# A weight block kept on chip, a gather ring of twelve buffers instead of four to six, and an output projection moved behind the first slots

## The chip, the cores and the metric

The kernel runs on one core of one Trainium2 chip. The metric is the device time in microseconds, lower is better. All data is float32.

## What is computed

One decoder layer over 256 tokens of width 1024: a mixer of two attention kinds (MoBA and FoX, 8 heads of 64 each), a cross attention over 256 memory tokens, then a PEER layer. The change touches the seam between the mixer's output projection and the PEER layer, which is this:

```python
def hybrid_mixer(...):
    ...
    o = jnp.concatenate([rmsnorm(o_a...), rmsnorm(o_b...)], axis=-1)
    return o @ w_out                                # 1024 x 1024

def peer_ffn(h, w_query, sub_keys_1, sub_keys_2, expert_down, expert_up):
    # per token: 8 heads, product keys (2 x 128 sub-keys), top 16 experts per head
    qr = (xc @ w_query).reshape(C, 8, 2, 64)
    s1 = einsum('chd,hnd->chn', qr[:, :, 0], sub_keys_1)
    s2 = einsum('chd,hnd->chn', qr[:, :, 1], sub_keys_2)
    v1, i1 = lax.top_k(s1, 16)
    v2, i2 = lax.top_k(s2, 16)
    ...                                             # top 16 of the 256 sums -> eidx, scores
    g = jax.nn.softmax(top_s, axis=-1)
    u = expert_down[eidx]                           # gathered rows of 1024
    a = gelu(einsum('cd,chkd->chk', xc, u))
    vv = expert_up[eidx]                            # gathered rows of 1024
    return einsum('chk,chkd->cd', g * a, vv)
```

Each of the 256 tokens needs 128 experts, each a row of expert_down and one of expert_up. The kernel reads both at once, as one row of 8 KB from `expert_rows`.

## The kernel before

The tokens are two tiles of 128 (T = 2, P = 128). The program has two parts. A list `main` of steps, written out by hand, takes both tiles through the attentions and tile 0 through everything up to its routing; then come 256 slots, 128 for each tile (SPT = 128). Every engine runs the same lists in the same order and does in each step what is its share; they meet only at semaphores.

A slot n handles one expert for each of the 128 tokens of a tile. GpSimd gathers 128 rows of 8 KB into a buffer of the ring (L551; 1.049 MB). VectorE's `dot(n)` multiplies the down half with the normalized token and sums (L1001). ScalarE's `weight(n)` makes gelu (L712), times the gate (L716), and a diagonal matrix `diag` from it (L719). TensorE's `up(n)` multiplies this with the up half and adds to the output in PSUM (L1291: 2 calls that the trace shows as 4 matmuls). That frees the buffer; `up_used` counts it. GpSimd waits for `up_used` of six slots back before it gathers into the same buffer (NS = 6; four of the buffers, NB = 4, lie in QKVB, two in SPARE).

During tile 0's 128 slots, tile 1's remaining stages are run between the slots. `slots` lists them: at which slot a stage stands, or at which four slots its four quarters stand. `after_slot(n, True)` gives TensorE's steps after up(n). `after_slot(n, False)` gives the shares of ScalarE and VectorE: those in OWN at the same slot, all others at the last slot of the stage plus LAG = 4. Names: wout = the mixer's output projection, xT = transposes for the cross attention, xq = its query, xS/xPT/xO = its scores, transposes, values, xo = its output projection, wq = the routing query in two halves of 512 columns, sc = the scores against the sub-keys. A key is (name, tile, half).

TensorE's products of these stages go to two PSUM banks for each of two groups (`v_jobs`, `a_jobs`), used in turn in the order of the steps. `bank_for` makes TensorE wait until the group's job two back has been emptied by ScalarE or VectorE (`freed`). wq, sc, xS, xPT and tile 1's xq are `a_jobs`, emptied by ScalarE; wout, xT, xO, xo are `v_jobs`, emptied by VectorE.

Weights come in blocks of 2 MB (512 columns) into six slots of W; `SLOT` says which, and a block waits until TensorE has done with the block before. The first half of the routing query's weights is loaded twice: early to SPARE (`wq_early`) for tile 0, and again to slot 0 of W for tile 1, after tile 1's wout half 0 (`main` ends with it). SPARE then becomes two buffers of the ring, once tile 0's wq half 0 is done.

The choice of experts for a head (`top_part`, VectorE, 16 parts) is spread over the slots of the head before. ScalarE adds a softmax to it (L704).

Of the kernel before, what the change touches and what calls it, by code (L numbers as in the profile page):

```python
# [18 lines left out]
D = 1024  # L19
# [41 lines left out]
def hybrid_layer(nc, A, out, bias_scratch):  # L61
# [7 lines left out]
    for name, cols in (("w_in", 6), ("w_xk", 2), ("w_xv", 2), ("w_out", 2), ("w_xq", 2), ("w_xo", 2),  # L69
                       ("w_peer_query", 2)):  # L70
        blocks += [(name, b) for b in range(cols)]

    SLOT = dict(zip(blocks, (0, 1, 2, 3, 4, 0, 1, 2, 3, 4, 0, 1, 2, 3, 4, MEM_SLOT, 0, 1)))
# [83 lines left out]
    for part in range(4):  # L157
# [17 lines left out]
    main += rest[1][1:] + [("wq", 0, 0), ("sc", 0, 0), ("sc", 0, 1)] + rest[0]  # L175


    slots = [((0, 1, 3, 4), ("wq", 0, 1)), (8, ("sc", 0, 2)), (9, ("sc", 0, 3)),
             (11, ("xT", 1, 0)), (11, ("xT", 1, 1)), (13, ("root_x", 1, 0)), (16, ("rstd_x", 1, 0)),
# [59 lines left out]
    with ctx:  # L239
# [85 lines left out]
        ROWS = [QKVB[:, 2 * i:2 * i + 2, :].rearrange("p a x -> p (a x)") for i in range(NB)]  # L325
        ROWS += [SPARE[:, 2 * i:2 * i + 2, :].rearrange("p a x -> p (a x)") for i in range(NS - NB)]

# [67 lines left out]
        row_in = [sem(f"row_in{i}") for i in range(NS)]  # L395
# [35 lines left out]
        def col(name, t, i):  # L431
            return {"root_m": i, "root_h": 2 + t, "o_root": 4 + 2 * t + i, "root_x": 8 + 2 * t,
                    "root_p": 9 + 2 * t, "root_y": 12 + t}[name]

# [16 lines left out]
        def _(sp):  # L451
# [63 lines left out]
            for b in (1, 0):  # L515
                load_block("w_peer_query", b)
# [10 lines left out]
        def _(pool):  # L527
# [29 lines left out]
        def _(act):  # L557
# [150 lines left out]
            def weight(n):  # L708

                i, H, k = n % NS, n // PK, n % PK  # L710
                act.wait_ge(dot_done, n + 1)
                nc.scalar.activation(gel[:, i:i + 1], dots[:, i:i + 1], ACT.Gelu, scale=rms("root_p", n // SPT)).then_inc(gelu_done, 1)  # L712
                act.wait_ge(gelu_done, n + 1)
                if k == 0:
                    act.wait_ge(gate_ready, H + 1)
                nc.scalar.activation(wgt[:, i:i + 1], gel[:, i:i + 1], ACT.Copy, scale=GATE[:, H % 3, k:k + 1])\  # L716
                    .then_inc(w_done, 1)
                act.wait_ge(w_done, n + 1)
                nc.scalar.activation(diag[:, i, :], ident[:, :], ACT.Copy, scale=wgt[:, i:i + 1])\  # L719
                    .then_inc(diag_done, 1)  # L720
# [20 lines left out]
        def _(dve):  # L741
# [255 lines left out]
            def dot(n):  # L997

                i = n % NS
                dve.wait_ge(row_in[i], 16 * (n // NS + 1))  # L1000
                nc.vector.tensor_tensor_reduce(out=ROWS[i][:, 0:D], in0=HP[n // SPT][:, :], in1=ROWS[i][:, 0:D],  # L1001
# [36 lines left out]
        def _(pe):  # L1038
# [64 lines left out]
            def step(name, t, i, part=None):  # L1103
# [146 lines left out]
                elif name in ("wq", "wq_first"):  # L1250
                    early = t == 0 and i == 0
                    w, bank = wq_early if early else wblk("w_peer_query", i), ab[AN[key] % 2]
                    if begins:
                        if early:
# [31 lines left out]
            def up(n):  # L1286
# [3 lines left out]
                for b in range(2):  # L1290
                    ins = nc.tensor.matmul(YP[t][:, b * BLK:(b + 1) * BLK], diag[:, i, :],  # L1291
                                           ROWS[i][:, D + b * BLK:D + (b + 1) * BLK], start=False,
# [39 lines left out]
```

## Time and profile before

| | |
|---|---|
| three runs | 932.72, 936.67, 942.36 us (median 936.67) |
| the profiled execution | 935.35 us, of which the span is 933.5 us |
| TensorE (PE) busy | 812.0 us, 87% of the span |
| VectorE (DVE) busy | 556.3 us, 60% |
| ScalarE (ACT) busy | 443.2 us, 47% |
| GpSimd (POOL) busy | 242.9 us, 26% |
| mean DMA rate | 339 GB/s over the span |

Slots run from about 276 us to 928 us. Engines: PE = TensorE matmul, PEld = its weight load, DVE = VectorE, ACT = ScalarE, POOL = GpSimd, SPq = SyncE's queue of transfers. A busy engine is not by itself the bound; what counts is which wait ends last in a stretch. In a row of the timeline "[0.77 <-ACT weights L699]" says that the engine was idle for 0.77 us before this, and that ScalarE's instruction of line 699 ended it.

### The profile page before, as it was taken

The numbers are of one execution on the slowest core, as the hardware profiler recorded it, in microseconds if no ns is written. First come the engines' busy times: TensorE is split into PE (matmuls) and PEld (weight loads), VectorE is DVE, ScalarE is ACT, GpSimd is POOL, SyncE is SP. The second block draws the span as 40 slices with busy tenths as digits, with TensorE's granted clock in tenths as the row PEclk, the third lists the DMA queues.
The fourth block names the chain that finished last, engine by engine and source line by source line (L and its number), as shares of the span: only waits on it lengthen the run. The fifth ranks groups of instructions, "written<-read, shape, count | busy, mean of one in ns | idle before, by whom it ended". The sixth has DMA issues, their size and how long they took to land.

```text
span 933.5 us, 9388 instructions
## 1 busy us (share of the span) xinstructions
PE 812.0 (87%) x3163; PEld 453.6 (49%) x3163; DVE 556.3 (60%) x1342; ACT 443.2 (47%) x1085; POOL 242.9 (26%) x267
## 2 busy tenths in 40 slices
PE   5999999999989899888899899977778787777885
PEld 3999897587555455344343456332223222222222
DVE  4464343212356766777768657776666666676543
ACT  4445555333324555565536644564553535445343
POOL 0000000000023333434333333433334343333430
PEclk9999999998999999999999999999999999999999
DMA  9749642052079999999999999999999999999994
GB/s 345 230 82 384 225 159 90 1 186 86 1 304 412 414 403 419 413 398 422 421 421 421 422 416 411 414 420 422 421 421 421 410 410 421 421 422 421 418 421 204
DMA packets 63299, 316.33 MB, mean 339 GB/s; under 512 B 7891, under 2 KB 10004, under 8 KB 30484
## 3 DMA queue, kind: packets, MB, share of 16 engines
q0 software_dynamic: 36864, 268.45, 69.6%
q1 hardware_dynamic: 26340, 47.28, 15.1%
q8 instruction: 25, 0.41, 0.2%
q14 instruction: 22, 0.18, 0.0%
q10 hardware_dynamic: 48, 0.01, 0.0%
HBM read 313.10 MB, written 2.62 MB: 338 GB/s over the span
## 4 chain that ended last, share of the span: by engine, by line
PE 49%; DMA 32%; ACT 10%; DVE 6%; issue 2%; SPq 0%; POOL 0%; POOLq 0%
DMA qkvb<-in_expert_rows,expert_idx 18%; DMA spare<-in_expert_rows,expert_idx 13%; PE y L1291 12%; PE v_bank L1291 6%; PE h_psum L1068 5%; PE v_bank L1061 4%; PE a_bank L1061 4%; PE a_bank L1068 4%; PE v_bank L1068 4%; PE h_psum L1061 3%; DVE qkvb L1001 3%; ACT diag L719 2%; ACT L712 2%; PE v_bank L1156 2%; DVE spare L1001 2%
## 5 line engine op out<-in xcount | busy, mean ns | idle before, releaser
L551 POOL DMA_INDIRECT qkvb<-in_expert_rows,expert_idx x172 | 161.7, 940 | 537.9 <-DVE expert_idx L984 262.6
L712 ACT ACTIVATE gelu<-dots,stat 128x1 f32<-128x1 f32 x256 | 75.2, 294 | 310.6 <-DVE dots L1001 310.1
L1291 PE MATMUL v_bank<-qkvb,diag 128*128 128x512 f32 x344 | 171.0, 625 | 47.8 <-ACT diag L719 47.8
L1291 PE MATMUL y<-qkvb,diag 128*128 128x512 f32 x344 | 162.7, 611 | 21.0 <-ACT diag L719 21.0
L1001 DVE CUSTOM_DVE_ANT_0 qkvb<-a_bank,qkvb 128x1024 f32<-128x1024 f32 x86 | 105.2, 1223 | 72.4 <-DMA qkvb<-in_expert_rows,expert_idx 72.3
L1001 DVE CUSTOM_DVE_ANT_0 qkvb<-h_psum,qkvb 128x1024 f32<-128x1024 f32 x86 | 105.0, 1223 | 62.4 <-DMA qkvb<-in_expert_rows,expert_idx 62.3
L1291 PEld LDWEIGHTS v_bank<-qkvb,diag 128*128 128x128 f32 x344 | 60.4, 192 | 157.9 <-ACT diag L719 110.1
L551 POOL DMA_INDIRECT spare<-in_expert_rows,expert_idx x84 | 79.7, 949 | 132.1 <-PE y L1291 67.9
L1291 PEld LDWEIGHTS y<-qkvb,diag 128*128 128x128 f32 x344 | 62.5, 192 | 101.4 <-issue 57.5
L719 ACT ACTIVATE diag<-ident,wgt 128x128 f32<-128x128 f32 x256 | 102.7, 401 | 8.3
L1291 PE MATMUL v_bank<-spare,diag 128*128 128x512 f32 x168 | 81.7, 613 | 21.6 <-ACT diag L719 21.6
L1291 PE MATMUL y<-spare,diag 128*128 128x512 f32 x168 | 79.7, 611 | 7.0 <-ACT diag L719 7.0
L716 ACT ACTIVATE wgt<-gelu,gates 128x1 f32<-128x1 f32 x256 | 75.4, 295 | 8.4
L1001 DVE CUSTOM_DVE_ANT_0 spare<-a_bank,spare 128x1024 f32<-128x1024 f32 x42 | 51.4, 1224 | 35.7 <-DMA spare<-in_expert_rows,expert_idx 35.7
L1001 DVE CUSTOM_DVE_ANT_0 spare<-h_psum,spare 128x1024 f32<-128x1024 f32 x42 | 51.3, 1221 | 25.4 <-DMA spare<-in_expert_rows,expert_idx 25.3
L1291 PEld LDWEIGHTS v_bank<-spare,diag 128*128 128x128 f32 x168 | 29.2, 189 | 73.3 <-ACT diag L719 50.1
L808 DVE TENSOR_TENSOR weights_r<-weights,spare_r 128x2048 fp32r<-128x2048 f32 x20 | 45.8, 2289 | 29.8 <-ACT spare_r L620 29.8
L1291 PEld LDWEIGHTS y<-spare,diag 128*128 128x128 f32 x168 | 30.6, 193 | 46.1 <-issue 27.2
L620 ACT CAST spare_r<-weights 128x2048 fp32r<-128x2048 f32 x20 | 38.0, 1898 | 22.2 <-PE v_bank L1068 21.3
L1061 PEld LDWEIGHTS a_bank<-x_and_h,weights 128*128 128x128 f32 x320 | 39.2, 193 | 11.2 <-issue 11.2
L1061 PE MATMUL a_bank<-x_and_h,weights 128*128 128x128 f32 x320 | 39.3, 276 | 0.8 <-ACT weights L699 0.8
L1068 PE MATMUL h_psum<-weights_r 128*128 128x256 f32 x128 | 36.1, 282 | 0.0
(200 smaller groups left out, 1135.4 us busy)
## 6 DMA issues: line engine op xcount, KB each, us to landing
weights<-in_w_in SPq DMA_DIRECT2D x6, 2048.0 KB, 13.5
weights<-in_w_xk SPq DMA_DIRECT2D x2, 2048.0 KB, 16.8
weights<-in_w_xv SPq DMA_DIRECT2D x2, 2048.0 KB, 17.8
weights<-in_w_out SPq DMA_DIRECT2D x2, 2048.0 KB, 8.8
weights<-in_w_xq SPq DMA_DIRECT2D x2, 2048.0 KB, 7.8
weights<-in_w_xo SPq DMA_DIRECT2D x2, 2048.0 KB, 11.0
weights<-in_w_peer_query SPq DMA_DIRECT2D x2, 2048.0 KB, 15.3
qkvb<-in_expert_rows,expert_idx POOLq DMA_INDIRECT x172, 10.0
```

The source lines that it names most:

```text
L551: pool.indirect_dma_start(ROWS[n % NS], None, expert_rows, bass.IndirectOffsetOnAxis(ap=IDX[:, H % 3, k:k + 1], axis=0))\
L620: act.copy(WH_r[t % 2], half_block(t, W)).then_inc(high_ready, 1)
L712: nc.scalar.activation(gel[:, i:i + 1], dots[:, i:i + 1], ACT.Gelu, scale=rms("root_p", n // SPT)).then_inc(gelu_done, 1)
L716: nc.scalar.activation(wgt[:, i:i + 1], gel[:, i:i + 1], ACT.Copy, scale=GATE[:, H % 3, k:k + 1])\
L719: nc.scalar.activation(diag[:, i, :], ident[:, :], ACT.Copy, scale=wgt[:, i:i + 1])\
L808: nc.vector.tensor_tensor(half_block(t, W_r), half_block(t, W), WH_r[t % 2].bitcast(f32), ALU.subtract).then_inc(low_ready, 1)
L1001: nc.vector.tensor_tensor_reduce(out=ROWS[i][:, 0:D], in0=HP[n // SPT][:, :], in1=ROWS[i][:, 0:D], scale=1.0, scalar=0.0, op0=ALU.mult, op ...
L1061: ins = nc.tensor.matmul(bank[:, lo:lo + n], lhs(k), rhs(k), start=(k == 0), stop=(k == chunks - 1))
L1068: ins = nc.tensor.matmul(bank[:, lo:lo + n], a(k), b(k), start=(k == 0 and p == 0), stop=(k == KC - 1 and p == 2))
L1156: ins = nc.tensor.matmul(bank[:, 0:nk], Q[lo:lo + HD, t, c, :], K[lo:lo + HD, 0:t + 1, c, :], start=True, stop=i < NH)
L1291: ins = nc.tensor.matmul(YP[t][:, b * BLK:(b + 1) * BLK], diag[:, i, :], ROWS[i][:, D + b * BLK:D + (b + 1) * BLK], start=False, stop=n % ...
```

## The change

Three edits. (1) The first half of the routing query's weights stays in SPARE for both tiles, and its second load goes. (2) The ring has twelve buffers: four in QKVB, and eight that become free in the course of tile 0's slots, two each after tile 1's wout half 0 (slot 0 of W), xq half 1 (second halves of slots 2 and 3 of W), the last xO (the memory keys and values), and wq half 0 (SPARE). Which buffer a gather takes is worked out in advance: the one that is free first. (3) Tile 1's wout half 0 moves from the end of `main` to slots 3 to 6. Tile 0's wq half 1 moves from slots 0 to 4 to slots 7 to 13, its scores from 8 and 9 to 18 and 19, xT from 11 to 12. Since dots, diag and the like still have six places, VectorE and ScalarE get a wait each for the place.

By these rules gathers 4 to 10 take the buffer of four slots back, 11 and 12 the two behind wout, 13 to 39 that of six slots back, 42 to 72 eight, 75 to 113 ten, 116 and on twelve.

```diff
@@ -68,9 +68,9 @@
-        blocks += [(name, b) for b in range(cols)]
-
-    SLOT = dict(zip(blocks, (0, 1, 2, 3, 4, 0, 1, 2, 3, 4, 0, 1, 2, 3, 4, MEM_SLOT, 0, 1)))
+        blocks += [(name, b) for b in range(cols) if (name, b) != ("w_peer_query", 0)]
+
+    SLOT = dict(zip(blocks, (0, 1, 2, 3, 4, 0, 1, 2, 3, 4, 0, 1, 2, 3, 4, MEM_SLOT, 1)))
@@ -172,11 +172,11 @@
-    main += rest[1][1:] + [("wq", 0, 0), ("sc", 0, 0), ("sc", 0, 1)] + rest[0]
-
-
-    slots = [((0, 1, 3, 4), ("wq", 0, 1)), (8, ("sc", 0, 2)), (9, ("sc", 0, 3)),
-             (11, ("xT", 1, 0)), (11, ("xT", 1, 1)), (13, ("root_x", 1, 0)), (16, ("rstd_x", 1, 0)),
+    main += rest[1][1:] + [("wq", 0, 0), ("sc", 0, 0), ("sc", 0, 1)]
+
+
+    slots = [((3, 4, 5, 6), ("wout", 1, 0)), ((7, 9, 11, 13), ("wq", 0, 1)), (18, ("sc", 0, 2)), (19, ("sc", 0, 3)),
+             (12, ("xT", 1, 0)), (12, ("xT", 1, 1)), (13, ("root_x", 1, 0)), (16, ("rstd_x", 1, 0)),
              ((19, 21, 23, 25), ("xq", 1, 0)), ((27, 29, 31, 33), ("xq", 1, 1))]
@@ -431,6 +428,26 @@
+        ROWS = [QKVB[:, 2 * i:2 * i + 2, :].rearrange("p a x -> p (a x)") for i in range(NB)]
+        ROWS += [W[:, wslot("w_out", 0), 2 * D * i:2 * D * (i + 1)] for i in range(2)]
+        ROWS += [W[:, wslot("w_xq", b), 2 * D:4 * D] for b in range(2)]
+        ROWS += [KM[:, :, :].rearrange("p c x -> p (c x)"), VM[:, :, :].rearrange("p a x -> p (a x)")]
+        ROWS += [SPARE[:, 2 * i:2 * i + 2, :].rearrange("p a x -> p (a x)") for i in range(2)]
+
+
+        last_of = dict(zip(range(NB, len(ROWS)), [st for st in (("wout", 1, 0), ("xq", 1, 1), ("xO", 1, XH_N - 1),
+                                                                ("wq", 1, 0)) for _ in range(2)]))
+        leaves = {st: at[-1] if isinstance(at, tuple) else at for at, st in slots}
+        free_from = {i: leaves[st] for i, st in last_of.items()}
+        BUF, USE, TAKES_FROM = [], [], []
+        for n in range(T * SPT):
+            before = {i: max([m for m in range(n) if BUF[m] == i], default=None) for i in range(len(ROWS))}
+            at = {i: before[i] if before[i] is not None else free_from.get(i, i - NB) for i in range(len(ROWS))}
+            i = min(at, key=lambda i: (at[i], i))
+            BUF.append(i)
+            USE.append(BUF.count(i))
+            TAKES_FROM.append(before[i])
@@ -512,8 +529,7 @@
-            for b in (1, 0):
-                load_block("w_peer_query", b)
+            load_block("w_peer_query", 1)
@@ -544,13 +560,13 @@
-                if n == NB:
-                    pool.wait_ge(a_full, AN[("wq", 0, 0)] + 1)
-                if n >= NS:
-                    pool.wait_ge(up_used, n - NS + 1)
-                pool.indirect_dma_start(ROWS[n % NS], None, expert_rows,
+                if TAKES_FROM[n] is not None:
+                    pool.wait_ge(up_used, TAKES_FROM[n] + 1)
+                elif BUF[n] in last_of:
+                    pool.wait_ge(*full(last_of[BUF[n]]))
+                pool.indirect_dma_start(ROWS[BUF[n]], None, expert_rows,
                                         bass.IndirectOffsetOnAxis(ap=IDX[:, H % 3, k:k + 1], axis=0))\
-                    .then_inc(row_in[n % NS], 16)
+                    .then_inc(row_in[BUF[n]], 16)
@@ -716,6 +732,8 @@
+                if n >= NS:
+                    act.wait_ge(up_used, n - NS + 1)
                 nc.scalar.activation(diag[:, i, :], ident[:, :], ACT.Copy, scale=wgt[:, i:i + 1])\
                     .then_inc(diag_done, 1)
@@ -997,8 +1015,11 @@
                 i = n % NS
-                dve.wait_ge(row_in[i], 16 * (n // NS + 1))
-                nc.vector.tensor_tensor_reduce(out=ROWS[i][:, 0:D], in0=HP[n // SPT][:, :], in1=ROWS[i][:, 0:D],
+                rows = ROWS[BUF[n]][:, 0:D]
+                dve.wait_ge(row_in[BUF[n]], 16 * USE[n])
+                if n >= NS:
+                    dve.wait_ge(gelu_done, n - NS + 1)
+                nc.vector.tensor_tensor_reduce(out=rows, in0=HP[n // SPT][:, :], in1=rows,
                                                scale=1.0, scalar=0.0, op0=ALU.mult, op1=ALU.add,
                                                accum_out=dots[:, i:i + 1]).then_inc(dot_done, 1)
@@ -1248,10 +1269,9 @@
-                    early = t == 0 and i == 0
-                    w, bank = wq_early if early else wblk("w_peer_query", i), ab[AN[key] % 2]
+                    w, bank = wq_early if i == 0 else wblk("w_peer_query", i), ab[AN[key] % 2]
...
```

## Rows read from the trace of the kernel before

**Rows 1.** The page: engines' busy time, and the gathers' DMA queue.
```profile
PE 812.0 (87%) x3163; PEld 453.6 (49%) x3163; DVE 556.3 (60%) x1342; ACT 443.2 (47%) x1085; POOL 242.9 (26%) x267
...
q0 software_dynamic: 36864, 268.45, 69.6%
```

**Rows 2.** Stretches: PE, PEld, DVE, ACT, POOL busy, PE clock, DMA share, GB/s.
```profile
320.00:330.00 10.00, 10.00 (x21) 4.38 (x20) 6.63 (x18) 5.63 (x15) 4.37 (x5) 0.83 0.99 379
...
600.00:740.00 140.00, 108.28 (x223) 39.36 (x223) 96.80 (x245) 71.37 (x189) 51.70 (x55) 0.99 1.01 421
```

**Rows 3.** Timeline, VectorE: dots of gathers 5, 8, 19, 20, 21, 39, 255.
```profile
285.53 1.23 DVE L1001 CUSTOM_DVE_ANT_0 spare<-h_psum,spare 128x1024 f32<-128x1024 f32 x1 [0.22 <-DMA spare<-in_expert_rows,expert_idx]
...
298.42 1.22 DVE L1001 CUSTOM_DVE_ANT_0 qkvb<-h_psum,qkvb 128x1024 f32<-128x1024 f32 x1 [1.19 <-DMA qkvb<-in_expert_rows,expert_idx]
...
325.51 1.22 DVE L1001 CUSTOM_DVE_ANT_0 qkvb<-h_psum,qkvb 128x1024 f32<-128x1024 f32 x1 [0.89 <-DMA qkvb<-in_expert_rows,expert_idx]
...
328.00 1.22 DVE L1001 CUSTOM_DVE_ANT_0 qkvb<-h_psum,qkvb 128x1024 f32<-128x1024 f32 x1 [0.73 <-DMA qkvb<-in_expert_rows,expert_idx]
...
332.50 1.23 DVE L1001 CUSTOM_DVE_ANT_0 qkvb<-h_psum,qkvb 128x1024 f32<-128x1024 f32 x1 [2.90 <-DMA qkvb<-in_expert_rows,expert_idx]
...
377.31 1.22 DVE L1001 CUSTOM_DVE_ANT_0 qkvb<-h_psum,qkvb 128x1024 f32<-128x1024 f32 x1 [0.57 <-DMA qkvb<-in_expert_rows,expert_idx]
...
923.11 1.22 DVE L1001 CUSTOM_DVE_ANT_0 qkvb<-a_bank,qkvb 128x1024 f32<-128x1024 f32 x1 [1.21 <-DMA qkvb<-in_expert_rows,expert_idx]
```

**Rows 4.** Timeline, SyncE's queue: the two loads of routing weights.
```profile
261.28 14.62 SPq L463 DMA_DIRECT2D weights<-in_w_peer_query  x2
```

**Rows 5.** Timeline: one round of a buffer in the second tile.
```profile
905.78 1.22 DVE L1001 CUSTOM_DVE_ANT_0 qkvb<-a_bank,qkvb 128x1024 f32<-128x1024 f32 x1 [1.26 <-DMA qkvb<-in_expert_rows,expert_idx]
...
908.16 1.98 PE L1291 MATMUL v_bank<-qkvb,diag 128*128 128x512 f32 x4 [0.51 <-ACT diag L719]
...
910.41 0.94 POOL L551 DMA_INDIRECT qkvb<-in_expert_rows,expert_idx  x1 [1.55 <-PE v_bank L1291]
```

**Rows 6.** Issues of gathers 0, 20, 21; landing times of the 0.5 MB loads.
```profile
265.07 1.09 POOL L551 DMA_INDIRECT qkvb<-in_expert_rows,expert_idx  x1 [262.63 <-DVE expert_idx L984]
...
321.32 0.94 POOL L551 DMA_INDIRECT qkvb<-in_expert_rows,expert_idx  x1 [4.47 <-PE y L1291]
...
324.23 0.94 POOL L551 DMA_INDIRECT qkvb<-in_expert_rows,expert_idx  x1 [1.97 <-PE y L1291]
...
DMA to landing us min/median/max: 3.3/3.8/4.2
```

**Rows 7.** Timeline, TensorE: end of main, the first slots, and after a wait.
```profile
267.18 1.26 PE L1277 MATMUL a_bank<-subkeys_t,scaled_gffn 64*128 64x128 f32 x12 [0.57 <-ACT scaled_gffn L689]
...
278.52 3.40 PE L1291 MATMUL y<-qkvb,diag 128*128 128x512 f32 x4 [3.01 <-ACT diag L719]
...
318.56 5.40 PE L1291 MATMUL y<-qkvb,diag 128*128 128x512 f32 x8 [2.91 <-ACT diag L719]
```

**Rows 8.** Chain that ended last: start, us; a v_bank quarter, an a_bank quarter, two up-projections.
```profile
458.66 1.72 PE v_bank L1061 x4
...
540.10 1.78 PE a_bank L1061 x16
541.89 3.44 PE y L1291 x8
```

**Rows 9.** Timeline around slot 112: dot, copy of scores, the quarter that waits.
```profile
562.42 1.23 DVE L1001 CUSTOM_DVE_ANT_0 spare<-h_psum,spare 128x1024 f32<-128x1024 f32 x1 [1.23 <-DMA spare<-in_expert_rows,expert_idx]
...
564.65 0.57 ACT L699 COPY weights<-a_bank 128x512 f32<-128x512 f32 x1
...
565.36 2.02 PE L1061 MATMUL a_bank<-x_and_h,weights 128*128 128x128 f32 x16 [0.77 <-ACT weights L699]
```

**Rows 10.** Timeline, VectorE: two dots that waited longer, gathers 124 and 227.
```profile
593.12 1.22 DVE L1001 CUSTOM_DVE_ANT_0 spare<-h_psum,spare 128x1024 f32<-128x1024 f32 x1 [1.62 <-DMA spare<-in_expert_rows,expert_idx]
...
853.61 1.22 DVE L1001 CUSTOM_DVE_ANT_0 spare<-a_bank,spare 128x1024 f32<-128x1024 f32 x1 [1.88 <-DMA spare<-in_expert_rows,expert_idx]
```

More of the change, by code:

```diff
@@ L323, in hybrid_layer @@
         sc = Ssb[:, 1, :].rearrange("p (a x) -> p a x", a=2)
-        ROWS = [QKVB[:, 2 * i:2 * i + 2, :].rearrange("p a x -> p (a x)") for i in range(NB)]
-        ROWS += [SPARE[:, 2 * i:2 * i + 2, :].rearrange("p a x -> p (a x)") for i in range(NS - NB)]
         wq_early = SPARE[:, :, :].rearrange("p a x -> p (a x)").rearrange("p (k c) -> p k c", k=KC)
@@ L394, in hybrid_layer @@
         top_in, top_exp, idx_ready, gate_ready = sem("top_in"), sem("top_e"), sem("idx_ready"), sem("gate_ready")
-        row_in = [sem(f"row_in{i}") for i in range(NS)]
+        row_in = [sem(f"row_in{i}") for i in range(NB + 8)]
         dot_done, gelu_done, diag_done, up_used = (sem("dot_done"), sem("gelu_done"), sem("diag_done"),
@@ L1250, in step @@
                 elif name in ("wq", "wq_first"):
-                    early = t == 0 and i == 0
-                    w, bank = wq_early if early else wblk("w_peer_query", i), ab[AN[key] % 2]
+                    w, bank = wq_early if i == 0 else wblk("w_peer_query", i), ab[AN[key] % 2]
                     if begins:
-                        if early:
+                        if i == 0:
                             pe.wait_ge(ld_early, 16)
@@ L1291, in up @@
                     ins = nc.tensor.matmul(YP[t][:, b * BLK:(b + 1) * BLK], diag[:, i, :],
-                                           ROWS[i][:, D + b * BLK:D + (b + 1) * BLK], start=False,
+                                           ROWS[BUF[n]][:, D + b * BLK:D + (b + 1) * BLK], start=False,
                                            stop=n % SPT == SPT - 1)
```

## The prediction

> **What bounds the kernel now.** The page comes first. TensorE is busy for 87% of the span and looks like the bound, but queue 0, which carries the expert rows, has moved 268.45 MB of the 316 MB [rows 1]. The table of stretches says more. From 600 to 740 us the share of the 16 DMA engines is 1.01 at 421 GB/s while TensorE is busy for 108 of 140 us [rows 2]: there the transfers bound the kernel. So I follow the landings, not an engine. A slot's dot product on VectorE starts where its gather lands, whenever the idle time before it ends with the DMA. A gather is 128 rows of 8 KB, 1.049 MB; at 421 GB/s that is 2.49 us, and gathers 19 and 20 land 2.49 us apart [rows 3]. I call 2.486 us the pitch and measure each landing by its offset, the time less 2.486 n:
>
> - gather 5: 285.53 - 12.4 = 273.1
> - gather 8: 298.42 - 19.9 = 278.5
> - gather 19: 325.51 - 47.2 = 278.3
> - gather 21: 332.50 - 52.2 = 280.3
> - gather 39: 377.31 - 97.0 = 280.4
> - gather 255: 923.11 - 634.0 = 289.1 [rows 3]
>
> A loop at its limit would keep the offset. All that any edit to the loop can win is in those 16.0 us: 5.4 from gather 5 to 8, 2.0 at gather 21, 8.7 after gather 39. From the last dot to the end of the span are 10.4 us, which the change leaves alone. The profiled execution took 935.35 us (1.3 below the median 936.67, 1.85 above its span 933.5).
>
> **The change, part by part.**
>
> The second load of the first half of the routing weights goes. SyncE issues both halves' loads in one group, 14.62 us from the first issue [rows 4]; the second runs beside gathers 5 to 8. Its 2.097 MB at 421.8 GB/s are 4.97 us, nearly all of the 5.4. Term: -5.4, if nothing else leaves the DMA engines idle there.
>
> Four buffers instead of six until slot 6. The two SPARE buffers now hold weights up to slot 103. By the diff's list gathers 4 to 10 each wait for the up-projection four slots back, 11 and 12 for the last quarter of the output projection in slot 6, 13 and on for that six slots back (eight from gather 42, ten from 75, twelve from 116). One round of a buffer: from the dot to the next issue 910.41 - 905.78 = 4.63 us [rows 5], then issue to landing. For the latter in an empty queue the trace has no clean row. Gather 20, issued 4.2 us before gather 19 landed, landed on pitch, 6.7 us after issue; gather 21, issued 3.8 us before gather 20, took 8.27 us and came 2.0 late [rows 3, 6]. A plain 0.5 MB load took 3.3 us at least [rows 6], so with another half megabyte (1.24 us) 4.5 is the lower end. I take 6.5, close to the row that kept its pitch, with 4.5 and 8.3 as ends. A round is then 4.63 + 6.5 = 11.1 us against 4 x 2.486 = 9.9.
>
> In times: gather 0 is issued at 265.07 [rows 6] and lands at 271.6, the next three follow on pitch. TensorE goes idle at 267.18 + 1.26 = 268.4, so its first up-projection runs slowly: 3.40 us, as now after a similar idle time, for 1.98 [rows 5, 7], 1.4 us more. Gather 4 is issued at 271.6 + 4.63 + 1.4 = 277.6 and lands at 284.1, 2.6 late. From slot 3 TensorE has an up-projection (3.44 / 2 = 1.72) and a quarter of the moved output projection (1.72, the row of a like one) in each slot [rows 8], 3.44 us for a pitch of 2.49: slot 4's up-projection ends at 288.4, slot 6's at 295.3, slot 6's quarter at 297.0. Gather 10 is issued at 295.5, lands at 302.0, 5.5 late, and gather 11 at 304.5. Offset 271.6 + 5.6 = 277.2, against 278.3 now. So the opening gives 1.1 us, not 5.4. Starting slot 0 without the 7.1 us of this projection ahead of it is in these times already. The matmuls move and none goes; VectorE's one add moves with them, to slot 10, where VectorE waits for landings anyway.
>
> A wait that the diff does not name. ScalarE's and VectorE's share of a stage follows LAG = 4 slots after TensorE's. The second routing half moves to slots 7 to 13, its two score products to slots 18 and 19. ScalarE thus empties the first one's bank after slot 22. But TensorE's step ("xq", 1, 0) in slot 19 writes that same bank (two jobs later, and there are two banks), and waits for it. Now the scores lie in slots 8 and 9, and the copy is done by slot 13. The trace has one wait of the kind: scores in slot 108, copied in slot 112, bank wanted in slot 111; TensorE resumes 565.36 - 562.42 = 2.94 us after the dot of slot 112 starts, 0.77 us idle [rows 9]. One slot ahead costs little; three slots ahead is two pitches more. Queued behind it are up-projections 20 to 22, and gathers 26 and on wait for those. Gather 22 lands at 277.2 + 54.7 = 331.9, TensorE resumes at 334.8 after some 6 us idle. It then has the quarter of xq (1.78) and up-projection 20 (1.72) before gather 26 goes out. After 2.9 us idle at 316 eight matmuls took 5.40 us where others take 3.44, and the granted clock of the stretch is 0.83 [rows 2, 7, 8], between full 2.4 GHz and a share at 1.2: I take 1.8 us more. So 340.1, issue at 340.3, landing at 346.8; on pitch it would be 341.8. Lost: 5.0 us. After that two slots cost TensorE 3.44 + 1.78 = 5.22 us [rows 8] against 4.97, so the backlog holds to slot 33, some five pairs, 1.2 us. Offset at gather 39: 277.2 + 5.0 + 1.2 = 283.4, against 280.4 now: **+3.0 us**.
>
> The Trainium skill, "DMA: Bandwidth & Descriptors", section "Anatomy of one DMA", fits a DMA issued from GpSimd as about 2.0 us + bytes / 436 GB/s, 4.4 us for this gather. No row here shows one so short. By it the gather round would be 9.0 us, under four pitches, and the bank wait would leave about 3 us; the sum would come out at 930. This is the second rival below, priced there from rows.
>
> The wider ring. Of the 8.7 us after gather 39, two transfers of 0.5 MB (the final gain, the first tile's output) are 2 x 1.24 = 2.5 by the pitch, and stay. The other 6.2 are small steps of at most 1.1 us. About half, 3.5, lie in the first tile, beside its stages, where TensorE or ScalarE gives a buffer back late; the one at gather 124 (593.12, idle 1.62 us) stands in [rows 10]. The rest lie in the second tile, which has no stages; gather 227's (853.61) stands there, 1.0 late, and a longer queue can't mend what no late buffer caused. Bounds: 0 to 3.5, and with no such distinction 6.2. I take two thirds of the first tile's: **-2.3 us**.
>
> At nothing: the new waits of ScalarE for up_used before writing diag and of VectorE for gelu_done, since six places of diag and dots were covered by the six buffers before, and ScalarE is half idle; GpSimd's waits, since each is for something older than the gather before; the first tile's experts for a head are ready nine slots ahead, which only caps the twelve at nine across a head's end.
>
> Sum: 935.35 + 3.0 - 2.3 = **936 us**.
>
> **Rivals.**
>
> 1. The bank wait is not there or is covered (ScalarE reaches slot 22 while TensorE is still behind). For it: TensorE's backlog from slots 3 to 13. Against: by my times TensorE has caught up by slot 19. Price: -6.2, so 930.
> 2. A gather into an empty queue lands after 4.5 us, not 6.5. It enters three times, in two rounds of four buffers and once after the bank wait: 936 - 6 = 930. Against it stand gathers 20 and 21.
> 3. Slower. It takes 8.3 us, as gather 21: 936 + 3 x 1.8 = 941; with the ring giving nothing back, 944. The one mechanism is DMA engines idle between slots 4 and 33. It is slower by over 1% (9.4 us) only from about 9.4 us per landing, which no row shows.
> 4. The wide ring holds the pitch throughout, every step outside the two transfers was a late issue: 16.0 - 2.5 = 13.5 us off, 922. Against: the steps of the second tile [rows 10].
>
> **How the numbers follow.** Chances: forecast 0.40, rival 1 0.16, rival 2 0.14, rival 3 0.22, rival 4 0.08. The predicted time is the forecast's. Range 928 to 943: below are rival 4 and little else, above the worst part of rival 3; it takes in 930 and 941 with two or three us for the median of a few runs, since the runs of before lie between 932.72 and 942.36. About 1% is what a measurement can tell from no change. Under 927.3: rival 4 and the edge of rivals 1 and 2, 0.13. Over 946: 0.09. Between: 0.78.
>
> **What would show it.** Gather 8's offset near 275 to 276 and the next ones rising to 277 by gather 11 (opening). In slot 19, near 328, TensorE idle about 6 us until ScalarE's copy of scores of shape 128x512; then DMA share below 1 in 335 to 345 and a landing about 5 us late at gather 26. Offsets level across slots 37 to 64 and at gather 124. The last dot 10.4 us before the end. Wrong if slot 19 shows no wait, if gathers 4 and 8 land on pitch, or if offsets after gather 39 rise by over 9 us or under 5.

## The result: slower by 0.7%

| | median | lowest to highest | runs |
|---|---|---|---|
| before | 935.84 us | 931.33 to 943.62 | 20 |
| after | 943.15 us | 938.44 to 948.40 | 20 |

The ratio is 1.0074, 95% interval 1.0056 to 1.0092, so about 7 us more. The profiled execution took 940.76 us with a span of 939.0. The median lies 7 us above the forecast of 936 and 0.15 us past the upper end of its range (943). One execution each of e2, e4 and e10 below, and one of before beside e1 to e4, was over 10% slower than the rest; the ratios leave these out.

The slots' landings show where. These are dots of the kernel after, on VectorE's timeline (start in us, duration, what ended the idle time before it): gathers 0, 4, 11, 25, 26, 27, 30, 32, 39 and 255.

```profile
268.97 1.23 DVE L1022 CUSTOM_DVE_ANT_0 qkvb<-h_psum,qkvb 128x1024 f32<-128x1024 f32 x1 [5.94 <-DMA qkvb<-in_expert_rows,expert_idx]
...
280.90 1.22 DVE L1022 CUSTOM_DVE_ANT_0 qkvb<-h_psum,qkvb 128x1024 f32<-128x1024 f32 x1 [2.33 <-DMA qkvb<-in_expert_rows,expert_idx]
...
302.71 1.22 DVE L1022 CUSTOM_DVE_ANT_0 weights<-h_psum,weights 128x1024 f32<-128x1024 f32 x1
...
337.46 1.23 DVE L1022 CUSTOM_DVE_ANT_0 qkvb<-h_psum,qkvb 128x1024 f32<-128x1024 f32 x1 [0.87 <-DMA qkvb<-in_expert_rows,expert_idx]
...
344.94 1.23 DVE L1022 CUSTOM_DVE_ANT_0 qkvb<-h_psum,qkvb 128x1024 f32<-128x1024 f32 x1 [5.52 <-DMA qkvb<-in_expert_rows,expert_idx]
...
349.14 1.23 DVE L1022 CUSTOM_DVE_ANT_0 qkvb<-h_psum,qkvb 128x1024 f32<-128x1024 f32 x1 [2.42 <-DMA qkvb<-in_expert_rows,expert_idx]
...
358.30 1.23 DVE L1022 CUSTOM_DVE_ANT_0 weights<-h_psum,weights 128x1024 f32<-128x1024 f32 x1 [1.83 <-DMA weights<-in_expert_rows,expert_idx]
...
365.16 1.22 DVE L1022 CUSTOM_DVE_ANT_0 qkvb<-h_psum,qkvb 128x1024 f32<-128x1024 f32 x1 [2.84 <-DMA qkvb<-in_expert_rows,expert_idx]
...
382.53 1.22 DVE L1022 CUSTOM_DVE_ANT_0 qkvb<-h_psum,qkvb 128x1024 f32<-128x1024 f32 x1 [0.58 <-DMA qkvb<-in_expert_rows,expert_idx]
...
928.55 1.22 DVE L1022 CUSTOM_DVE_ANT_0 qkvb<-a_bank,qkvb 128x1024 f32<-128x1024 f32 x1 [1.23 <-DMA qkvb<-in_expert_rows,expert_idx]
```

The offset (time less 2.486 n) is 275.4 at gather 11 and still 275.3 at gather 25, as in [rows 3] a landing every 2.486 us. It is 280.3 at gather 26, 282.0 at 27, 283.7 at 30 and 285.6 at 32. Then it is level to gather 39 and reaches 294.6 at the last.

The instructions before the slots are nearly the same in all kernels, yet the first gather goes out at a different time in each execution: at 265.07 us in the profile of before [rows 6], at 262.38 here, between 260.8 and 268.1 in the others. I therefore compare the offset less the time of the first issue, which I call the lag:

| lag, us | gather 19 | 25 | 32 | 39 | 255 | rise from 39 to 255 |
|---|---|---|---|---|---|---|
| before | 13.2 | 15.3 | 15.3 | 15.3 | 24.1 | 8.8 |
| after | 13.0 | 12.9 | 23.2 | 23.2 | 32.2 | 9.0 |

So 10.3 us go between gathers 25 and 32. At gather 25 the kernel after was still 2.4 us ahead of before, so 7.9 remain at gather 39, beside the 7 us of the medians. Each lag is from one profiled execution, and it varies: e3 and e6 below have this kernel's instructions up to slot 18 and show 15.3 and 13.4 at gather 19 for the 13.0 here. A difference of 2 us between two profiles is therefore no more than a hint; the 10.3 us are a rise within one.

Around slot 19 the timeline of TensorE and its neighbours reads as follows: the second score product, the dot of slot 22, ScalarE's copy of the first score product, the quarter of the cross-attention query that waits for it, the next up-projections, and GpSimd's issue of gather 26.

```profile
327.39 1.16 PE L1297 MATMUL a_bank<-subkeys_t,scaled_gffn 64*128 64x128 f32 x8
...
330.05 1.23 DVE L1022 CUSTOM_DVE_ANT_0 qkvb<-h_psum,qkvb 128x1024 f32<-128x1024 f32 x1 [0.59 <-DMA qkvb<-in_expert_rows,expert_idx]
...
332.28 0.57 ACT L715 COPY x_and_h<-a_bank 128x512 f32<-128x512 f32 x1
...
332.99 3.76 PE L1082 MATMUL a_bank<-x_and_h,weights 128*128 128x128 f32 x16 [4.45 <-ACT x_and_h L715]
...
336.54 4.24 PE L1311 MATMUL y<-qkvb,diag 128*128 128x512 f32 x8
...
339.33 0.94 POOL L567 DMA_INDIRECT qkvb<-in_expert_rows,expert_idx  x1 [10.66 <-PE y L1311]
```

TensorE stood idle for 4.45 us, until ScalarE had made the copy that comes after the dot of slot 22. It resumed 2.94 us after that dot started, as in [rows 9]; there it had to wait for the next slot only, here for the one three slots on. Then the quarter took 3.76 us for the usual 1.95. GpSimd had nothing free to gather into for 10.66 us, and the last of its gathers had landed 1.9 us before it issued the next. The stretches (PE, PEld, DVE, ACT, POOL busy, PE clock, DMA share, GB/s) show the DMA engines idle for a third of the time, a granted clock of 0.77 on average, and, less expected, that they move only 384 GB/s in the 30 us behind it, at a share of 1.00:

```profile
330.00:345.00 15.00, 12.01 (x47) 8.35 (x48) 7.44 (x18) 4.93 (x15) 2.33 (x3) 0.77 0.64 244
345.00:375.00 30.00, 30.00 (x142) 19.24 (x141) 16.70 (x45) 10.44 (x32) 11.66 (x13) 1.00 1.00 384
```

### The profile page after: what moved, and what is told of

Same layout as the page of the kernel before. It is cut to its first block, busy times and chain, and to the rows that moved or that the text cites. A ratio compares the mean times of both kernels' runs of the same rounds, so it can differ in the third digit from the quotient of the medians.

```text
span 939.0 us, 9886 instructions
## 1 busy us (share of the span) xinstructions
PE 813.3 (87%) x3163; PEld 453.9 (48%) x3163; DVE 556.5 (59%) x1342; ACT 443.0 (47%) x1085; POOL 242.8 (26%) x267
## 4 chain that ended last, share of the span: by engine, by line
DMA 44%; PE 42%; ACT 6%; DVE 4%; issue 3%; POOL 1%; SPq 0%; DVEq 0%; POOLq 0%
DMA weights<-in_expert_rows,expert_idx 29%; DMA spare<-in_expert_rows,expert_idx 11%; PE y L1311 10%; PE h_psum L1089 5%; PE a_bank L1089 4%; PE v_bank L1082 4%; PE v_bank L1089 4%; DMA qkvb<-in_expert_rows,expert_idx 3%; PE a_bank L1082 3%; PE v_bank L1311 3%; PE h_psum L1082 3%; PE v_bank L1177 2%; PE y L1198 1%; ACT diag L737 1%; DMA weights<-in_w_in 1%
## 5 line engine op out<-in xcount | busy, mean ns | idle before, releaser
L567 POOL DMA_INDIRECT qkvb<-in_expert_rows,expert_idx x110 | 103.7, 942 | 422.1 <-DVE expert_idx L1002 261.3
L1311 PE MATMUL y<-qkvb,diag 128*128 128x512 f32 x264 | 126.7, 613 | 15.0 <-ACT diag L737 14.9
L567 POOL DMA_INDIRECT weights<-in_expert_rows,expert_idx x90 | 84.9, 943 | 149.1 <-PE y L1311 69.5
L1311 PE MATMUL v_bank<-weights,diag 128*128 128x512 f32 x172 | 89.0, 641 | 27.4 <-ACT diag L737 27.4
L1311 PE MATMUL v_bank<-qkvb,diag 128*128 128x512 f32 x176 | 86.0, 616 | 20.0 <-ACT diag L737 20.0
L1311 PE MATMUL y<-weights,diag 128*128 128x512 f32 x188 | 91.3, 612 | 12.6 <-ACT diag L737 12.6
L1022 DVE CUSTOM_DVE_ANT_0 weights<-h_psum,weights 128x1024 f32<-128x1024 f32 x47 | 57.5, 1223 | 31.2 <-DMA weights<-in_expert_rows,expert_idx 31.1
L1022 DVE CUSTOM_DVE_ANT_0 qkvb<-a_bank,qkvb 128x1024 f32<-128x1024 f32 x44 | 53.9, 1224 | 37.2 <-DMA qkvb<-in_expert_rows,expert_idx 37.2
L1022 DVE CUSTOM_DVE_ANT_0 weights<-a_bank,weights 128x1024 f32<-128x1024 f32 x43 | 52.6, 1224 | 37.6 <-DMA weights<-in_expert_rows,expert_idx 37.6
L1311 PE MATMUL v_bank<-spare,diag 128*128 128x512 f32 x80 | 39.2, 614 | 8.4 <-ACT diag L737 8.4
L1082 PEld LDWEIGHTS a_bank<-x_and_h,weights 128*128 128x128 f32 x256 | 32.6, 200 | 12.9 <-issue 12.9
## 6 DMA issues: line engine op xcount, KB each, us to landing
weights<-in_w_in SPq DMA_DIRECT2D x6, 2048.0 KB, 13.4
weights<-in_w_xk SPq DMA_DIRECT2D x2, 2048.0 KB, 17.3
```

The source lines that it names most:

```text
L567: pool.indirect_dma_start(ROWS[BUF[n]], None, expert_rows, bass.IndirectOffsetOnAxis(ap=IDX[:, H % 3, k:k + 1], axis=0))\
L1022: nc.vector.tensor_tensor_reduce(out=rows, in0=HP[n // SPT][:, :], in1=rows, scale=1.0, scalar=0.0, op0=ALU.mult, op1=ALU.add, accum_out=d ...
L1082: ins = nc.tensor.matmul(bank[:, lo:lo + n], lhs(k), rhs(k), start=(k == 0), stop=(k == chunks - 1))
```

## The experiments

All are float32 kernels of the same work. Each was timed in five rounds beside the kernel before; a ratio is to that, with its 95% interval. The lags are read from each one's profile as above, one profile for each.

| run | ratio | lag at 19 | 25 | 32 | 39 | rise 39 to 255 |
|---|---|---|---|---|---|---|
| e1, scores early | 1.0050 (1.0027 to 1.0073) | 18.6 | 20.8 | 20.8 | 20.8 | 10.3 |
| e2, before, scores late | 1.0059 (1.0033 to 1.0085) | 13.0 | 13.0 | 21.4 | 22.0 | 8.2 |
| e3, xq four later | 0.9981 (0.9953 to 1.0009) | 15.3 | 15.9 | 16.3 | 16.2 | 10.7 |
| e4, wout in main | 1.0006 (0.9978 to 1.0034) | 13.1 | 13.6 | 13.6 | 13.6 | 10.9 |
| e5, e4 with six buffers | 0.9998 (0.9979 to 1.0018) | 14.1 | 15.7 | 17.3 | 17.3 | 14.0 |
| e6, after with six buffers | 1.0078 (1.0051 to 1.0105) | 13.4 | 13.3 | 22.2 | 22.1 | 11.6 |
| e7, e4, add after the dots | 0.9954 (0.9925 to 0.9983) | 9.4 | 11.2 | 12.3 | 12.3 | 9.2 |
| e8, e7 with six buffers | 0.9964 (0.9939 to 0.9990) | 8.4 | 9.9 | 9.9 | 9.8 | 11.0 |
| e9, e8 less the added waits | 0.9957 (0.9932 to 0.9981) | 8.6 | 9.5 | 9.5 | 9.4 | 10.7 |
| e10, before with the added waits | 0.9999 (0.9976 to 1.0022) | 13.4 | 15.6 | 15.6 | 15.5 | 13.1 |

### The bank wait, taken away and put in

Run e3_xq_four_later moves the step that waits:

```diff
-             ((19, 21, 23, 25), ("xq", 1, 0)), ((27, 29, 31, 33), ("xq", 1, 1))]
+             ((23, 25, 27, 29), ("xq", 1, 0)), ((31, 33, 35, 36), ("xq", 1, 1))]
```

> The changed kernel with the other end of the wait moved: tile 1's cross-attention query from slots 19 to 33 to slots 23 to 36, four buffers at the start and the late scores kept. Theory 1: no wait (the bank is copied after slot 22), offset at gather 39 about 276 to 278, time 934 to 936. Rivals A and B: 943.

Measured: 934.59 us, ratio 0.9981; against the changed kernel's 1.0074 that is 0.9%, 8 to 9 us. After the second score product TensorE goes on at once (its timeline; then the stretch as above):

```profile
333.11 1.16 PE L1297 MATMUL a_bank<-subkeys_t,scaled_gffn 64*128 64x128 f32 x8
...
343.02 1.95 PE L1082 MATMUL a_bank<-x_and_h,weights 128*128 128x128 f32 x16
```
```profile
330.00:345.00 15.00, 13.75 (x54) 7.56 (x54) 10.19 (x25) 9.43 (x23) 5.62 (x6) 1.00 1.01 421
```

The DMA engines are full in those 15 us, and the lag rises by 0.3 us from gather 25 to 32 instead of 10.3. The offset at gather 39 was 281.9, not 276 to 278: the first gather went out 3.3 us later than in the profile of after, and the same opening lost 2.4 us more. The opening with four buffers, the late scores and the ring of twelve are all still there.

Run e2_before_scores_late does the same part alone in the kernel before:

```diff
-    slots = [((0, 1, 3, 4), ("wq", 0, 1)), (8, ("sc", 0, 2)), (9, ("sc", 0, 3)),
+    slots = [((0, 1, 3, 4), ("wq", 0, 1)), (18, ("sc", 0, 2)), (19, ("sc", 0, 3)),
```

> The kernel before with one thing of the change alone: the scores moved from slots 8 and 9 to 18 and 19; reload, six buffers and everything else stay. Theory 1: TensorE waits 4 to 6 us in slot 19, gathers 26 to 32 come late, plus 8 to 10 us, ratio 1.009 to 1.011. Rivals A and B: no more than 1 us, ratio within 1.001.

In this kernel root_x writes its unused squares over the query (both use XS) before the late scores read it, so heads 4 to 7 of tile 0 choose other experts; the amount of work is the same. Measured: 942.25 us, ratio 1.0059. TensorE waits for the bank in the same place and as long:

```profile
336.50 3.75 PE L1061 MATMUL a_bank<-x_and_h,weights 128*128 128x128 f32 x16 [4.42 <-ACT x_and_h L699]
```

The lag rises by 8.4 us from gather 25 to 32. The time rose by 5.5 us (3.1 to 8.0 by the interval), less than the 8 to 10 expected. The profile of before has a step of 2.0 us at gather 21 [rows 3] that this one lacks (lag 13.0 at gather 25, for 15.3), so that 6.7 us remain at gather 39. Taking the wait out of the changed kernel gives back 8 to 9 us, and putting it into the one before costs 5.5: the wait, with what follows it, is the cause of the slowdown.

### Why the scores had been moved

Run e1_scores_early puts them and the routing half back into the changed kernel:

```diff
-    slots = [((3, 4, 5, 6), ("wout", 1, 0)), ((7, 9, 11, 13), ("wq", 0, 1)), (18, ("sc", 0, 2)), (19, ("sc", 0, 3)),
+    slots = [((3, 4, 5, 6), ("wout", 1, 0)), ((0, 1, 3, 4), ("wq", 0, 1)), (8, ("sc", 0, 2)), (9, ("sc", 0, 3)),
```

> The changed kernel with one thing put back: the second routing half in slots 0, 1, 3, 4 and its scores in slots 8 and 9, as before the change. Theory 1 (the bank wait of slot 19 and the backlog behind it cost the loop about 10 us: the offset rose from 275.35 at gather 25 to 285.6 at gather 32): no wait in slot 19, offset at gather 39 near 276 to 278 (slots 3 and 4 now carry two quarters each), time about 934 to 936, ratio to before 0.998 to 1.001. Rival A (the opening with four buffers is the loss, the wait is covered): within 1 us of the changed kernel's 943. Rival B (twelve buffers, or rows in other places of the memory, make the landings slower): also 943.

Measured: 942.59 us. The wait is gone, but the 934 to 936 did not come, and by time alone this run would have spoken for the four buffers. The lag says what happened: it is 18.6 already at gather 19 and 20.8 at gather 25, and flat after that. Slots 3 and 4 now hold two quarters each, and with four buffers GpSimd waits for each up-projection behind them (timeline; the issues of gathers 8 and 9 with the quarters ahead):

```profile
290.10 1.88 PE L1311 MATMUL y<-qkvb,diag 128*128 128x512 f32 x4
291.82 1.88 PE L1082 MATMUL v_bank<-weights,x_and_h 128*128 128x512 f32 x4
292.26 0.94 POOL L567 DMA_INDIRECT qkvb<-in_expert_rows,expert_idx  x1 [4.28 <-PE y L1311]
293.54 1.95 PE L1082 MATMUL a_bank<-x_and_h,weights 128*128 128x128 f32 x16
295.32 1.88 PE L1311 MATMUL y<-qkvb,diag 128*128 128x512 f32 x4
297.04 1.88 PE L1082 MATMUL v_bank<-weights,x_and_h 128*128 128x512 f32 x4
297.48 0.94 POOL L567 DMA_INDIRECT qkvb<-in_expert_rows,expert_idx  x1 [4.28 <-PE y L1311]
```

Two issues 5.2 us apart where a landing takes 2.49: two quarters and an up-projection occupy TensorE for that long. In e3, with the quarters spread as in the changed kernel, the lag at gather 11 is 15.4, here 18.6. So in this opening the quarters have to be spread, and the spreading is what put the scores late. One loss was exchanged for another that is nearly as large. Whether six buffers would ride over the double quarters was not run.

### Where the reload's 5 us are

Run e4_wout_in_main undoes the third edit: the projection back ahead of slot 0, wq, scores and xT at their old slots; no reload, six buffers from the start and twelve later.

```diff
-    main += rest[1][1:] + [("wq", 0, 0), ("sc", 0, 0), ("sc", 0, 1)]
+    main += rest[1][1:] + [("wq", 0, 0), ("sc", 0, 0), ("sc", 0, 1)] + rest[0]
...
+        leaves["wout", 1, 0] = -1
```

> The changed kernel with its third edit undone: the output projection stays ahead of slot 0, the second routing half in slots 0 to 4, scores in 8 and 9, xT in 11. The reload stays away, the ring has six buffers from the start and twelve later. Theory 1 together with the 5.0 us of the reload: no wait, offset at gather 8 about 3 to 4 below that of the kernel before, time 931 to 933, ratio 0.995 to 0.997. If the reload only filled DMA time that the opening leaves idle anyway: 935 to 936, ratio 1.0. Rival B: above 936.

Measured: 936.82 us, ratio 1.0006, by the ratio the second of the three cases. Its lag at gather 19 is 13.1, that of before 13.2: the reload was a transfer in time that the opening leaves idle otherwise. The stretch behind the first slots shows it, e4 first and then before:

```profile
280.00:300.00 20.00, 20.00 (x91) 12.79 (x90) 15.12 (x50) 9.28 (x24) 5.62 (x6) 0.92 0.93 338
280.00:300.00 20.00, 20.00 (x93) 12.98 (x92) 13.05 (x44) 8.19 (x21) 5.69 (x7) 0.94 1.02 412
```

VectorE's add of the projection stands ahead of dot 0, so the first up-projection starts at 279.13 after 3.01 us of idle time and takes 3.29 us, as in [rows 7], and gather 6 waits for it. Run e7_add_after_dots moves that one add:

```diff
             for st in whole(main, 3):
-                step(*st)
+                if st != ("wout", 1, 0):
+                    step(*st)
...
                 dot(n)
+                if n == 3:
+                    step("wout", 1, 0)
```

> Run e4_wout_in_main with one more edit: VectorE's add of the output projection comes after the dot of slot 3 and not ahead of slot 0, so that the first dots start as their gathers land (near 272) and TensorE goes from the projection (ends near 275.5) straight into slot 0, without idle time or low clock. In e4 the freed time of the reload was lost in the opening: offset less the first issue 13.1 at gather 19, as before the change. If the late start of the first round does this: gather 6 is issued near 277.5 and not 282.7, offset less first issue 9 to 11 at gather 19, time 2 to 4 us below e4. If six buffers beside the quarters of slots 0 to 4 do it: same as e4 within 1 us.

Measured: 932.51 us, ratio 0.9954, the fastest with e8 and e9. The projection (7.13 us) goes into slot 0's up-projection without a gap and without the low clock, the first dots run as their gathers land, and gather 6 is issued at 273.98, 13.2 us after gather 0; in before it was 17.1 after. The lag at gather 19 is 9.4.

```profile
264.09 7.13 PE L1086 MATMUL v_bank<-weights,x_and_h 128*128 128x512 f32 x16
...
267.58 1.23 DVE L1023 CUSTOM_DVE_ANT_0 qkvb<-h_psum,qkvb 128x1024 f32<-128x1024 f32 x1 [6.15 <-DMA qkvb<-in_expert_rows,expert_idx]
...
271.06 1.88 PE L1315 MATMUL y<-qkvb,diag 128*128 128x512 f32 x4
...
273.98 0.93 POOL L568 DMA_INDIRECT qkvb<-in_expert_rows,expert_idx  x1 [0.31 <-issue]
```

So the two edits together, no reload and the later add, are worth some 4 us, and the first alone nothing that the time shows. What the later add would give with the reload kept was not run. An estimate from these profiles: in e7 the lag is 6.7 us at gather 3 and 9.4 from gather 4 on, since gather 4 waits for the projection's buffer; with the reload's 4.97 us on top of the 6.7 instead it would be 11.7, against 13.2 in before. By that the later add would win 1.5 us of the 3.8 and the reload's absence 2.3.

### The ring

Three pairs differ only in the ring: e5, e6 and e8 have six buffers throughout where e4, the changed kernel and e7 have twelve.

```diff
-            i = min(at, key=lambda i: (at[i], i))
+            i = min([i for i in at if i < 6], key=lambda i: (at[i], i))
```

> Run e4_wout_in_main with the ring held at six buffers throughout (four in QKVB, two in slot 0 of W); all else equal. Theory 2 (a ring beyond six buffers saves nothing, and lets the offset rise faster: 10.9 us from gather 39 to 255 in e4 against 8.7 and 8.2 in the two kernels with six buffers): the rise is 7 to 9 us, time 1 to 3 us below e4, ratio to before 0.996 to 0.999. Theory 3 (the ring of twelve keeps the transfers fed across the stages): the rise is 12 us or more, time above e4's.

> The changed kernel with the ring held at six buffers; the opening with four, the late scores and the bank wait kept. Both theories expect the wait of slot 19 and some 10 us of offset from gather 25 to 32. Theory 2: rise after gather 39 of 7 to 9 us, time the same as the changed kernel or up to 2 us below, 941 to 943. Theory 3: 945 or more.

> Both edits of e5 and e7: wout in main, its add after the dot of slot 3, six buffers throughout. If both act: 3 to 6 us below e4, ratio to before 0.993 to 0.996, the fastest of all. If neither: as e4, ratio 1.000.

Measured, six buffers against twelve: 935.67 against 936.82 us (ratios 0.9998 and 1.0006), 944.07 against 943.15 (1.0078 and 1.0074), 932.51 against 932.51 (0.9964 and 0.9954). In the times the ring makes no difference that can be told, but with intervals of about 0.2 to 0.3% on each ratio, 2 to 3 us, a gain of the size forecast isn't excluded either. In the profiles the rise from gather 39 to 255 is 14.0 against 10.9, 11.6 against 9.0, 11.0 against 9.2, so it is 1.8 to 3.2 us smaller with twelve buffers, all three times against theory 2, which is out. That the ring saves these 1.8 to 3.2 us is not shown. One profile of each stands behind it; kernels with the same ring of twelve and the same slots after 39 lie between 9.0 and 10.9 (after, e1, e4, e7); and of the profiled executions those of e5 and e6 took 3.1 and 3.8 us more than their medians, those of e4 and after 0.6 and 2.4 us less.

### What the rise after gather 39 is

In the five kernels with twelve buffers it comes, in the second tile, in steps of about 1 us at the same gathers each time (142, 167, 189, 213, 238), with 22 us of issued gathers queued; a late issue can't be the cause there. Here are gathers 167, 189 and 213 of the kernel after:

```profile
707.03 1.22 DVE L1022 CUSTOM_DVE_ANT_0 weights<-a_bank,weights 128x1024 f32<-128x1024 f32 x1 [1.52 <-DMA weights<-in_expert_rows,expert_idx]
...
762.70 1.22 DVE L1022 CUSTOM_DVE_ANT_0 weights<-a_bank,weights 128x1024 f32<-128x1024 f32 x1 [1.85 <-DMA weights<-in_expert_rows,expert_idx]
...
823.32 1.23 DVE L1022 CUSTOM_DVE_ANT_0 weights<-a_bank,weights 128x1024 f32<-128x1024 f32 x1 [1.84 <-DMA weights<-in_expert_rows,expert_idx]
```

Within 10 us of each of the three the DMA table of that stretch has a transfer of the instruction queue 14, though others of its transfers have no step beside them. Over the span there are 26 of them after and 22 before (the page's queue lines, before and then after), and the program has 9886 instructions for 9388; the new waits are most of the difference.

```profile
q14 instruction: 22, 0.18, 0.0%
```
```profile
q14 instruction: 26, 0.21, 0.1%
```

Two runs ask whether these waits cost time. e9 leaves both out, which a ring of exactly six doesn't need; e10 adds both to the kernel before.

```diff
+                if n >= NS:
+                    act.wait_ge(up_used, n - NS + 1)
...
+                if n >= NS:
+                    dve.wait_ge(gelu_done, n - NS + 1)
```

> Run e8_add_after_dots_six without the change's two added waits per slot (ScalarE for up_used, VectorE for gelu_done), which a ring of exactly six buffers does not need. Theory 4 (the steps of about 0.95 us that come at fixed gathers, 167, 189, 213, 238 in every kernel with the changed slot code whatever its ring, are the fetching of instructions, and some 500 added waits bring more of them): the steps move and get fewer, the rise of the offset from gather 39 to 255 falls from 11.0 to about 9, time 1 to 2 us below e8. If the steps have nothing to do with the code's length: rise 10 to 11 and the same time as e8.

> The kernel before with nothing but the change's two added waits per slot, which its ring of six fulfils anyway. Theory 4: the steps of the second tile move to gathers near 142, 167, 189, 213, 238, rise from gather 39 to 255 about 10.5 to 11 for 8.8, time 1 to 2 us above before, ratio 1.001 to 1.002. If the waits cost nothing: rise 8 to 9, ratio 1.000.

Measured: 932.23 against e8's 932.51, and 936.70 against 935.78 beside it, ratio 0.9999. The waits cost nothing that can be measured, though e10's interval (2 us either way) does not exclude the 1 to 2 us of theory 4. But they do move the steps: e9, with 22 transfers of queue 14 again, has steps in the second tile at gathers 171, 203 and 227, where before has them (0.4, 1.0 and 0.5 us, for 0.9, 0.7 and 1.0), beside others at 209 and 241. e10, with 26, has those at 213 and 238, but none at 167. The fit is not complete: e2, with the slots of before, shows only the one at 227. e9's rise (10.7, expected 9) and e10's (13.1, expected 10.5 to 11) don't fit the sizes; the profiled execution of e10 took 3.7 us more than its median, so its rise doesn't measure what the waits cost. That the steps belong to places in the program is shown for the ring of twelve; that fetching instructions causes them fits and is not shown; how much of the rise it is stays open.

## Why the forecast was off

**The bound** was read rightly: landings at a pitch of 2.486 us in every run, and a change to the time is a change to the lag at some gather.

**The reload** was rightly found to be worth little in this opening. Forecast: offset 5.6 us above that of gather 0 from gather 11 on; measured 275.4 - 269.0 = 6.4. Gather 4 was 2.0 late (2.6 forecast), and took 5.5 us from issue to landing, gather 26 5.6, where 6.5 was taken. So the opening came out 0.8 us worse than forecast: the lag at gather 25 is 12.9, by the forecast 277.2 - 265.07 = 12.1. Against the 15.3 of before, 2.4 us were won and not 3.2.

**The step at gather 21** is 2.0 of these 2.4, and here the forecast had luck. It carried 277.2 on to gather 25 and gave no reason why the step of before [rows 3] should go. In before TensorE waits 2.91 us for a diag until 318.56 and then runs slowly, 5.40 us for eight matmuls [rows 7], and the next gathers go out late. The profiles differ in this. e7 and e8 have the same instructions there and almost the same wait:

```profile
310.42 5.40 PE L1315 MATMUL y<-qkvb,diag 128*128 128x512 f32 x8 [2.22 <-ACT diag L738]
```
```profile
310.30 3.70 PE L1315 MATMUL y<-qkvb,diag 128*128 128x512 f32 x8 [2.20 <-ACT diag L738]
```

From 309 to 316 us the granted clock is 0.76 on average in e7 and 1.00 in e8, and only e7 has the step (1.4 us, at gather 21). Before, e1, e5, e7 and e10 ran slowly after this wait and lost 1.4 to 2.1 us at gather 20 or 21; e2, e4, e8 and e9 waited 2.2 to 3.3 us, ran at the full clock and lost nothing; after, e3 and e6 don't have the wait. So 2.0 of the 15.3 us of before belong to its one profiled execution; how often its other executions have them isn't known.

**The bank wait** was where it was forecast, with gather 26 280.3 - 275.3 = 5.0 us late (5.0). Its parts differed: TensorE idle 4.45 us, not 6, and the low clock cost 1.8 us in the quarter alone (3.76 for 1.95) and 0.6 in the two up-projections behind it (4.24 for 3.60).

**The step that failed** is the one after it, "the backlog holds to slot 33, some five pairs, 1.2 us". It was 285.6 - 280.3 = 5.3 us. I had priced it from TensorE's surplus alone, 5.22 for 4.97 us in two slots. TensorE kept that pace, and gathers 26 to 33 were issued 17.4 us apart, 2.49 each; but they landed 22.7 us apart, 3.24 each. With issues at the pitch and landings slower than it, the loss is in the transfers: gathers 27 to 30 and 32 went out only 3.9 to 5.4 us before their predecessor landed (their lead), and the DMA engines moved 384 GB/s for 421. No other traffic was in the way: from 335 to 372 us queue 0 moved 11.81 of the 11.86 MB. Here are the issue of gather 30 and the dot of 29, the issue of 32 and the dot of 31:

```profile
349.77 0.94 POOL L567 DMA_INDIRECT weights<-in_expert_rows,expert_idx  x1 [2.56 <-PE y L1311]
...
354.70 1.23 DVE L1022 CUSTOM_DVE_ANT_0 weights<-h_psum,weights 128x1024 f32<-128x1024 f32 x1 [1.45 <-DMA weights<-in_expert_rows,expert_idx]
...
355.50 0.94 POOL L567 DMA_INDIRECT qkvb<-in_expert_rows,expert_idx  x1 [3.07 <-PE y L1311]
...
360.75 1.22 DVE L1022 CUSTOM_DVE_ANT_0 qkvb<-h_psum,qkvb 128x1024 f32<-128x1024 f32 x1 [0.79 <-DMA qkvb<-in_expert_rows,expert_idx]
```

The price behind it, that a gather issued 4.2 us ahead still lands on pitch, came from one row, gather 20 of [rows 3, 6]; gather 21 beside it, 3.8 ahead and 2.0 late, was the better guide. In the kernel after leads of 4.9 to 5.4 us cost 0.6 to 1.9 at gathers 29, 30 and 32, and the lag was level from gather 33 on, with leads of 6.9 and more. e2 and e6 have the same tail, 4.2 and 4.4 us more between gathers 26 and 39.

It isn't a fixed price. Gathers 28 (4.6 us ahead) and 20 (5.3 ahead) of the same profile kept the pitch. Over all twelve profiles, counting the dots that waited for their gather from gather 5 on, the share that came more than 0.3 us late falls with the lead:

| issued before the predecessor landed | late, of all |
|---|---|
| 3.5 to 4 us | 16 of 17 |
| 4 to 5 us | 28 of 61 |
| 5 to 6 us | 30 of 191 |
| 6 to 7 us | 23 of 377 |
| 7 us and more | 92 of 2117 |

That a short lead goes with late landings is shown; why one gather pays and the next doesn't is open, and no run changed the lead alone.

**The ring** (-2.3 us) is the second miss: the rise is 9.0 for 8.8. In the first tile, where the gain was forecast, it is smaller (3.3 us from gather 39 to 124, for 4.5), and level from gather 39 to 64 as foretold; in the second tile it is larger (5.8 from 124 to 255, for 4.3), with five steps at the program's fixed places for three. The pairs with six and twelve buffers leave open whether the ring gives anything in time. The first tile's small steps, which I had put down to late buffers, are at most partly that.

The sum by measured terms, as lag at gather 39: before 15.3; 2.4 less up to gather 25, 5.0 more for gather 26 and 5.3 for the tail make 23.2. That is 7.9 for the 3.0 forecast: 4.1 of the 4.9 missed are the tail (5.3 for 1.2), 0.8 the opening. With nothing back from the ring it makes some 8 us between the profiles, for the forecast 0.7 and the 7 of the medians. Rival 1 (no wait) and rival 2 (a landing in 4.5 us) are out; of rival 3 the place was right, gathers starved between slots 4 and 33, and its mechanism, one long landing in an empty queue, was not: landings in an empty queue were shorter than taken, those in a thin queue cost more. That its 941 to 944 hold the measured time is luck. The rule weighed in the forecast, 2.0 us + bytes / 436 GB/s of the Trainium skill ("DMA: Bandwidth & Descriptors", "Anatomy of one DMA"), gives an estimate of 4.4 us. The two landings in an empty queue here took 5.5 and 5.6, issue to dot. They decide, and lie about midway between the rule and the price taken.

## What to carry to other kernels

When a product is moved in a hand-written order, follow its PSUM bank to the next user and count from where the bank is emptied, not from where it is written: with evacuations a fixed number of slots behind, two moves that are each harmless can meet. A transfer that is taken away pays only if the transfers behind it can come forward; here the time showed a gain only when the consumer started early as well. And where a ring of buffers is refilled by its consumer, price a stall with its tail: here the stall's 5.0 us had a tail of another 5.3 until the gathers were issued some 7 us ahead again. A step that a profile shows in one execution may be missing in the next; before pricing it, look for it in a second one.

## What was not expected of the hardware

- A queue that was not empty but thin did not run at full rate: 384 GB/s from 345 to 375 us with two or three gathers of 1.049 MB queued and a DMA share of 1.00, against 421.
- A gather into an empty queue took 5.5 to 5.6 us from issue to dot (gathers 4 and 26), of which 2.49 are the pitch.
- After nearly the same wait (2.22 and 2.20 us) of the same instructions TensorE ran eight matmuls in 5.40 us in one execution and in 3.70 in another; the granted clock was 0.76 and 1.00.
- With twelve buffers, steps of about 1 us in the landings stayed at the same gathers through changes of the opening (five kernels); most of those of e8 moved when its added waits were left out (e9).
- The start of the first gather varied from 260.8 to 268.1 us between executions whose code ahead of it is all but the same.
